# Gate and up projection of an encoder layer: 2x2 blocks with seven block products in place of eight

## The reference

```
h = modulate(rms_norm(x, g_pre_ffn), sh2, sc2)
f = (jax.nn.silu(h @ w_gate) * (h @ w_up)) @ w_down
x = x + gt2[:, None] * rms_norm(f, g_post_ffn)
```

## Time and profile before

| | |
|---|---|
| median of 3 runs | 1005.39 us (1005.0 to 1005.47) |
| profiled execution, first to last instruction (span) | 1003.3 us |
| its own time | not listed; the median lies 2.1 us above its span |
| gate and up, 40 chunks | 592.71 to 848.06 us of the span |
| busy: PE, DVE, ACT, POOL | 95%, 44%, 41%, 36% of the span |

### The profile page before, as it was taken

The page is one execution under the profiler, slowest core; times in us unless marked ns, Lnnn a source line. Parts: engine busy times, 40 slices in busy tenths (PEclk is TensorE's granted clock), DMA queues, the critical chain, the costliest instruction groups (busy, mean ns, idle before and its releaser), DMA issues. The chain is left out here.

```text
span 1003.3 us, 17736 instructions
## 1 busy us (share of the span) xinstructions
PE 954.9 (95%) x7104; PEld 908.1 (91%) x7104; DVE 436.6 (44%) x871; ACT 412.6 (41%) x771; POOL 365.1 (36%) x174
## 2 busy tenths in 40 slices
PE   3899999999999999999999899999999999999995
PEld 1698898999998999988888799999999999999995
DVE  5767559988884323432102743333333332000005
ACT  4755335465556555543333932222222223222221
POOL 2031016456453231244443044444444442434440
PEclk9999999999999999999999999999999999999998
DMA  9821031232131114357865032222222212222202
GB/s 363 319 99 48 8 107 71 102 105 92 67 120 53 36 43 151 146 204 277 286 209 163 1 105 85 84 84 84 82 84 71 79 61 86 87 88 87 81 36 95
DMA packets 35600, 111.61 MB, mean 111 GB/s; under 512 B 4240, under 2 KB 9360, under 8 KB 35280
## 3 DMA queue, kind: packets, MB, share of 16 engines
q1 hardware_dynamic: 31152, 102.48, 29.4%
q10 hardware_dynamic: 4112, 6.93, 1.8%
q0 software_dynamic: 272, 1.31, 0.3%
HBM read 100.38 MB, written 10.32 MB: 110 GB/s over the span
## 5 line engine op out<-in xcount | busy, mean ns | idle before, releaser
L1108 POOL TENSOR_TENSOR wlo<-raw,whi 128x1024 fp32r<-128x1024 f32 x52 | 128.6, 2473 | 233.3 <-ACT whi L744 223.9
L1163 POOL TENSOR_TENSOR wlo<-raw,whi 128x1024 fp32r<-128x1024 f32 x41 | 104.7, 2555 | 151.2 <-ACT whi L1071 151.2
L1875 PE MATMUL pj<-hh,wlo 128*128 128x288 f32 (+1 forms) x640 | 137.3, 296 | 0.0
L1875 PE MATMUL pj<-hh,whi 128*128 128x288 f32 (+1 forms) x640 | 137.0, 295 | 0.0
L1875 PE MATMUL pj<-hl,whi 128*128 128x288 f32 (+1 forms) x640 | 136.8, 295 | 0.0
L1631 PE MATMUL pj<-hh,whi 128*128 128x288 f32 x544 | 124.4, 310 | 5.4 <-ACT zs L825 2.4
L1631 PE MATMUL pj<-hh,wlo 128*128 128x288 f32 x544 | 117.7, 298 | 0.0
L1631 PE MATMUL pj<-hl,whi 128*128 128x288 f32 x544 | 117.1, 297 | 0.0
L1875 PEld LDWEIGHTS pj<-hh,wlo 128*128 128x128 f32 x640 | 103.4, 189 | 0.0
L1875 PEld LDWEIGHTS pj<-hh,whi 128*128 128x128 f32 x640 | 102.9, 188 | 0.0
L1875 PEld LDWEIGHTS pj<-hl,whi 128*128 128x128 f32 x640 | 102.8, 188 | 0.0
(11 more groups left out here) (226 smaller groups left out, 1992.0 us busy)
## 6 DMA issues: line engine op xcount, KB each, us to landing
raw<-in_w_s SPq DMA_DIRECT2D x94, 512.0 KB, 3.5
rawa<-in_w_ada SPq DMA_DIRECT2D x32, 512.0 KB, 6.2
rawd<-in_w_d SPq DMA_DIRECT2D x16, 704.0 KB, 4.0
raw<-in_w_ada SPq DMA_DIRECT2D x16, 512.0 KB, 10.2
g_raw<-gz ACTq DMA_DIRECT2D x16, 288.0 KB, 2.1
gate<-g_raw SPq DMA_DIRECT2D x8, 576.0 KB, 3.8
rawv<-in_w_v SPq DMA_DIRECT2D x8, 324.0 KB, 5.1
xt<-in_xT SPq DMA_DIRECT2D x2, 1152.0 KB, 6.8
```

What stands on the lines that cost most here:

```text
L1108: pool.tensor_tensor(rest, raw_of(c), whole.bitcast(F32), ALU.subtract).then_inc(w_lo, 1)
L1163: pool.tensor_tensor(wlo[:, slot(c), :], raw[:, raw_slot(c), :], whi[:, slot(c), :].bitcast(F32), ALU.subtract).then_inc(w_lo, 1)
L1875: ins = mm(pj[tile % 2][:, h, 0:HALF + 2 * h], w[:, slot(C_GU + q), b:b + P], x[h][:, kc, :], start=(kc == 0 and w is whi and x is hh2), s ...
```

## The change

The chunk pair of a tile is taken as 2x2 blocks: rows gate and up, columns the two halves of the contraction (A11, A12 of gate, A21, A22 of up, each 128 x 512 numbers); `h` as 2x2 blocks: rows the halves of the contraction, columns the two token halves (B11 to B22). The four blocks of the result (gate and up for each token half) come from seven block products of sums of blocks, each 4 blocks x 3 matmuls of 290 columns, in place of eight. Tiles 0 and 1 (four chunks, `N_STD`) stay as they were; the other 20 (`N_PAIR`) go the new way.

- DVE makes four sums of weight blocks a tile (`weight_sum`, 128 x 512), and once four sums of token blocks (`t_make`) and their low parts (`t_rest`); ACT makes the high parts of those (`t_split`).
- ACT and POOL split the seven weight operands of a tile, 128 x 512 each (`operand_hi`, and the loop on POOL), into a pair of slots of their own for each product (`op_hi[k]`, `op_lo[k]`).
- Each product has a bank of its own. ACT copies the first one out; DVE adds the others up (`gate_up`), multiplies by `rstd2` after that, and makes f with three multiply-adds.
- f of tiles 2 to 21 is kept whole (`fx`). Its high and low parts are made at the end of the stretch (`f_whole` on ACT, `rest_of_f` on DVE), in places that become free there.
- The loops of the stretch are written out; SP loads two chunks a tile into two pairs of raw slots; w_down has slots of its own, loaded when the last low part of the weights is made. The squares of the last norm go through three slots.

```diff
+PRODUCTS = (("A11", "B11"), ("S2", "T2"), ("A12", "B21"), ("S1", "T1"), ("S3", "T3"), ("A22", "T4"), ("S4", "B22"))
...
+        def operand_free(eng, i, k):
+
+            if i:
+                eng.wait_ge(st_full, made(i - 1, k))
...
+            for i in range(N_PAIR):
+                for m in range(2):
+                    if i < 2:
+                        sp.wait_ge(pj_full, full(T_OUT + KC - 1))
+                    else:
+                        sp.wait_ge(st_lo, made(i - 2, N_PROD - 1))
+                    sp.dma_start(sraw[:, 2 * (i % 2) + m, :], a["w_s"][S_OUT + KC + N_STD + 2 * i + m])\
+                      .then_inc(sraw_in[2 * (i % 2) + m], 16)
...
+            def operand_hi(i, k):
+
+                src = operand(act, i, k)
+                operand_free(act, i, k)
+                act.activation(op_hi[k][:, :], src, ACT.Copy).then_inc(st_hi, 1)
...
+            def copy_p1(i):
+
+                act.wait_ge(st_full, made(i, 0))
+                if i:
+                    act.wait_ge(c21_c22, i)
+                act.activation(vbuf[:, 1, :], tb[:, 0:HX], ACT.Copy).then_inc(p1_out, 1)
...
+            for i in range(N_PAIR):
+                if i:
+                    silu(i - 1)
+                copy_p1(i)
+                if i + 1 < N_PAIR:
+                    for k in range(N_PROD):
+                        operand_hi(i + 1, k)
+            hi_down(0, 0)
+            f_whole(0, 4)
             hi_down(0, 1)
+            f_whole(4, 12)
+            silu(N_PAIR - 1)
+            f_whole(12, FC)
...
+            for i in range(N_PAIR):
+                for k in range(N_PROD):
+                    src = operand(pool, i, k)
+                    pool.wait_ge(st_hi, made(i, k))
+                    operand_free(pool, i, k)
+                    pool.tensor_tensor(op_lo[k][:, :], src, op_hi[k][:, :].bitcast(F32), ALU.subtract).then_inc(st_lo, 1)
...
+            def weight_sum(i, j):
+
+                a11, a12, a21, a22 = (sraw_of(i, m, k) for m in range(2) for k in range(2))
+                x, y, op = ((a21, a22, ALU.add), (ssum[:, 0, :], a11, ALU.subtract), (a11, a21, ALU.subtract),
+                            (a12, ssum[:, 1, :], ALU.subtract))[j]
...
+            def f_made(t, gate_, up_):
+
+                v.wait_ge(sg_ready, t + 1)
...
+                    parts = [(fx[t][:, 0:NS], up_[:, 0, 0:NS], gate_[:, 0:NS], up_[:, 1, HALF + 1:HX]),
+                             (fx[t][:, NS:HALF], up_[:, 0, NS:HALF], gate_[:, NS:HALF], up_[:, 1, HALF:HALF + 1]),
+                             (fx[t][:, HALF:T], up_[:, 1, 0:HALF], gate_[:, HALF:T], up_[:, 1, HALF:HALF + 1])]
+                for to, x, y, shift in parts:
+                    ins = v.scalar_tensor_tensor(out=to, in0=x, scalar=shift, in1=y, op0=ALU.add, op1=ALU.mult)
...
+            def gate_up(i):
+
+                u2 = gbuf[:, 0, :].unsqueeze(1).to_broadcast([P, 2, HX])
+                v.wait_ge(p1_out, i + 1)
+                v.wait_ge(st_full, made(i, 2))
+                v.wait_ge(sg_ready, i + 2)
+                v.tensor_tensor(gbuf[:, 0:2, :], vbuf[:, 1, :].unsqueeze(1).to_broadcast([P, 2, HX]), lg[:, :, 0:HX],
+                                ALU.add).then_inc(u2_c11, 1)
+                if i:
+                    f_made(i + 1, gt, up)
+                if i < N_PAIR - 1:
+                    weight_sum(i + 1, 2)
+                    weight_sum(i + 1, 3)
+                else:
+                    rest_of_f(0, 6)
+                v.wait_ge(st_full, made(i, 4))
+                v.wait_ge(u2_c11, i + 1)
+                v.tensor_tensor(vbuf[:, :, :], u2, pj4[:, 1:3, 0:HX], ALU.add).then_inc(u4_u3, 1)
+                v.wait_ge(st_full, made(i, 5))
+                v.wait_ge(u4_u3, i + 1)
+                if i:
+                    v.wait_ge(f_ready, i + 2)
+                v.tensor_tensor(up[:, :, :], vbuf[:, 1, :].unsqueeze(1).to_broadcast([P, 2, HX]), pj4[:, 0:2, 0:HX],
+                                ALU.add).then_inc(c21_c22, 1)
+                v.wait_ge(c21_c22, i + 1)
+                v.tensor_tensor(up[:, :, 0:HALF], up[:, :, 0:HALF], two(rstd2[:, :]), ALU.mult).then_inc(up_ready, 1)
+                v.wait_ge(st_full, made(i, 6))
+                v.tensor_tensor(gbuf[:, 2, :], vbuf[:, 0, :], pvb[:, 0:HX], ALU.add).then_inc(c12_out, 1)
+                v.wait_ge(c12_out, i + 1)
+                v.tensor_tensor(two(gt[:, :]), gbuf[:, 1:3, 0:HALF], two(rstd2[:, :]), ALU.mult).then_inc(gt_ready, 1)
+                v.wait_ge(up_ready, i + 1)
+                if i + 2 < N_PAIR:
+                    weight_sum(i + 2, 0)
+                    weight_sum(i + 2, 1)
...
+            def product(i, k):
+
+                pe.wait_ge(st_lo, made(i, k))
+                bank = (tb, lg[:, 0, :], lg[:, 1, :], pj4[:, 1, :], pj4[:, 2, :], pj4[:, 0, :], pvb)[k]
+                if i:
+                    pe.wait_ge((p1_out, u2_c11, u2_c11, c21_c22, u4_u3, c21_c22, c12_out)[k], i)
...
+                for b in range(KH):
+                    for j, (w, x) in enumerate(((op_hi, 0), (op_hi, 1), (op_lo, 0))):
+                        ins = mm(bank[:, 0:HX], w[k][:, b * P:(b + 1) * P], moving[name][x][:, b, :],
+                                 start=(b == 0 and j == 0), stop=(b == KH - 1 and j == 2))
+                ins.then_inc(st_full, 1)
+
+            for i in range(N_PAIR):
+                for k in range(N_PROD):
+                    product(i, k)
+            pe.wait_ge(c21_c22, N_PAIR)
```

More of the change, by code:

```diff
@@ L53 @@
 BLK_DOWN = FC // 2
+KH = KC // 2
+N_STD = 4
+N_PAIR = FC - N_STD // 2
+HX = HALF + 2
 QCOL = [0] + [NS + P * i for i in range(4)]
@@ L283, in build @@
         wlo, _ = sb("wlo", [P, RING, 1024], F32R)
[L285 to L288, removed]
         h_off = at["x"]
@@ L291, in build @@
         hl, _ = sb("hl", [P, KC, T], F32R)
[L292 to L295, removed]
+        at["x"] += 4 * KC * 2 * 4
+        off_l2 = h_off + 2 * KC * HX * 4
+        xres = [sb(f"xres{h}", [P, KC, HALF], where=off_l2 + h * KC * HX * 4)[0] for h in range(2)]
         A0 = at["x"]
@@ L549, in wait_used @@
                 tile = tile_of[c]
-            eng.wait_ge(pj_full, full(tile) if turns is None else turns * chunks + full(tile))
+            eng.wait_ge(pj_full, full(tile))
         def slot_free(eng, c):
@@ L1052, in hi_down @@
             def hi_down(d, k):
                 act.wait_ge(down_in[k], 16 * (d + 1))
[L1054 to L1079, removed]
+                if d:
+                    wait_down(act, d - 1, k)
+                else:
+                    act.wait_ge(st_lo, made(N_PAIR - 1, N_PROD - 1))
+                    act.wait_ge(st_full, made(N_PAIR - 1, k))
+                act.activation(dhi[k][:, :], rawd[:, k, :], ACT.Copy).then_inc(d_hi, 1)
+            def f_whole(t0, t1):
+                for t in range(t0, t1):
+                    act.wait_ge(f_ready, t + 1)
+                    act.wait_ge(st_full, made(N_PAIR - 1, FH_AFTER[t]))
+                    act.activation(fh[t][:, :], fx[t][:, :], ACT.Copy).then_inc(f_hi, 1)
@@ L1517, in _ @@
                     inverse(rstd1, 0, 1)
-                half_lo(h, 5, 6, 7)
+                    half_lo(h, 5, 6, 7)
+                else:
+                    for j in range(3):
+                        half_lo(h, 5 + j)
+                        weight_sum(0, j)
             def first_half(h):
@@ new lines, in _ @@
+            inverse(rstd2, 1, 0)
+            first_half(0)
+            t_make(0)
+            t_make(1)
+            inverse(rstd2, 1, 1)
+            first_half(1)
+            t_make(2)
+            weight_sum(0, 3)
+            v.wait_ge(pj_dve, taken(T_GU + 1, "D"))
+            f_made(0, sg, ft)
+            t_make(3)
+            t_rest(0)
+            n = T_GU + 2
+            v.wait_ge(pj_full, full(n))
+            v.wait_ge(f_ready, 1)
+            v.tensor_tensor(two(sg[:, :]), pj_view(n), two(rstd2[:, :]), ALU.mult)
```

380 lines of the change are left out of this document (254 added, 126 removed).

## The result

The changed kernel takes 1032.72 us (median of 4 runs, 1031.35 to 1033.42), the kernel before 1005.21 beside it (1005.0 to 1005.47): a ratio of 1.0272, 95% interval 1.0257 to 1.0286. The forecast was 1036.0. The profiled execution has a span of 1030.6 us against 1003.3, so 27.3 us have to be found.

The account below looks back on a forecast made before the run. VectorE, taking turns with GpSimd's low parts, was to set the tiles' pace instead of TensorE. Span 1003.3 + 16.2 (tiles) + 13.5 (seam) + 1.7 (clock) = 1034.7, plus 2.1 around it, 1036.8; forecast 1036 us, range 1004 to 1050.

Parts of the forecast that it names:

- The matmuls: In the 20 tiles: seven products for eight, 84 matmuls of 133.0 ns, 1.60 us less a tile, 31.9 us over all.
- The turn: VectorE's round per tile: 5.95 us of waits behind low parts plus 7.7 of own work, 13.7 us; given 70%.
- The stretch: The 20 gate and up tiles: 13.8 + 11.2 + 18 x 13.7 = 271.6 us against 255.35, +16.2 us.
- The seam: Ahead of the down projection: TensorE stands 13.7 us, with splits of f queued before two PSUM sums on VectorE; +13.5 us.
- The clock: Behind the wait ahead of the down projection: half of 3.4 us at half clock, +1.7 us; inside tiles hidden by waits.
- least port time: Per tile, GpSimd low parts (8.05 us) and VectorE operations with two SBUF inputs (4.1) taking turns without gaps: 12.15 us.
- the locked order of three engines: In the tiles: silu waits for VectorE, high parts queue behind silu, so low parts start with the multiply-adds; 13.7 us, not 12.15.
- TensorE keeping the pace: Rival in the tiles: low parts and two-input operations hardly meet, 11.2 us a tile, 977 us in all; 8%.
- The packed port: Rival in the tiles: the three multiply-adds go through together, VectorE's round about 12.4 us, 1013 us in all; 16%.
- Everything colliding: Rival in the tiles: all seven low parts stand in VectorE's way, 16.7 us a tile, 1100 us in all; 6%.

Follow-up runs that it names:

- e1_no_low: Changed kernel with GpSimd writing zeros in place of the weights' low parts from the second of the 20 tiles on: 984.8 us, ratio 0.9802.
- e2_seam: Changed kernel with the first six splits of f behind the last two PSUM sums in VectorE's queue: 1029.18 us, ratio 1.0239.
- e4: Changed kernel with the seven low parts of a tile made by VectorE instead of GpSimd from the second tile on: 1003.11 us, ratio 0.9976.
- v6: Changed kernel with prompt silu, up sum and C12 in PSUM, half the gate scaling reading PSUM, early splits of f behind the last tile's work: 983.87 us.
- e3: Changed kernel with ScalarE writing silu of the prompt tokens to PSUM, where two multiply-adds read it: 1004.3 us, ratio 0.9993.
- e5_order: Changed kernel with ScalarE's silu of a tile behind the first two high parts of the next: 1042.68 us, ratio 1.0369.

## Why the prediction was right, step by step

**The matmuls.** 1680 came, at 133.9 ns (11.25 us a tile in e1_no_low) where 133.0 was taken. Right within 0.1 us a tile, and off the path, as the forecast had it.

**The turn.** Forecast 13.7 us, measured 13.56 to 13.62 from the third turn on. Its inside fits as well: the waits over the price alone are 1.03 + 1.04 + 1.03 us for the multiply-adds (1541, 1486, 1309 less 512, 446, 280), 2 x (1250 - 685) = 1.13 for S3, 1.02 for the scaling of up and 0.60 for that of gate: 5.85 us where 5.95 stood in the sum. What is left, 7.74, is the own work taken as 7.7; the 0.2 us for marks in it, for which the forecast had no row, compare with 0.25 us a turn in which VectorE is not busy at all. Low parts and two-input operations at their full durations, 9.0 and 5.4 us, would add up to 14.4 us a turn, which did not come: the small overlaps seen in the earlier trace rows counted. That TensorE waits for the last PSUM sum ahead of the fourth product was right too; in tiles that ran at full clock the trace lists 1.76 us of idle time there (about 0.55 in those that had half clock before it). Start to start a tile is 13.59 - 11.25 = 2.34 us longer than its matmuls, and 2.5 was forecast. In many tiles some 0.26 us of that stands ahead of the first product, where the weight load does wait for GpSimd's low part (eight times from 640 to 810 us, 2.4 us in all); it costs nothing, as the fourth product has to wait anyway.

**The stretch: right mechanism, too long.** Forecast +16.2 us, measured +12.0. Of the 4.2 us: the first product began at 590.76, 1.95 us ahead of the 592.71 from which I counted. That is no gain of the change but chance: in the seven other versions, with the same work ahead, it began anywhere from 590.8 to 593.4. Up to the fourth product it took 6.36 us for the 4.8 of three products, as the second one waited 1.26 us for its block sum, which the sum did not have (+1.6). The first turn took 12.93 for 13.8 (-0.9): the sixth product waited 1.44 us where the term said 2.6, so the start waited 2.7 us in two places where the term had 2.6 in one. The second turn took 12.29 for 13.7 (-1.4): the lag had not built up yet. Seventeen turns at 13.59 for 13.7 are -1.8, the last four products +0.3.

**The seam.** Forecast 13.7 us of standing, measured 13.54. Its parts came as listed: first low part 861.98 to 865.15, first split behind it to 865.76, second low part to 868.78 with a split behind it, the others to 872.07, the two sums to 873.59. e2_seam shows what the order is worth: not all 13.5, but 7.8 at the first wait and 3.5 in the end.

**The clock.** +1.7 was forecast behind the seam, half of the 3.4 us at a granted clock of 0.50 in the earlier trace rows; that it would last as long behind the seam no row showed. The down projection took 2.1 longer. The term was too small, as the half clock lasted 5.7 us there (0.51 from 873.64 to 879.40). Inside the tiles the forecast let the clock fall into time that is waited anyway. That held: in five tiles it was at half for 3.4 us (0.50 from 637.0 to 640.4), and the turn stayed at 13.6.

**A reason that stays open.** The forecast laid the gap between the least port time (12.15) and the turn (13.7) on the locked order of three engines, low parts let go just when the multiply-adds start. GpSimd does wait for high parts, 49.4 of 170 us. The runs don't part order from load. e1, e4 and v6 shorten the turn by taking readers off the port. In e3 the port time falls too, but most of the gain is a smaller gap above it, and GpSimd waits for 12.0 of 170 us: that speaks for the order. e5_order, the one run that changes the order alone, moved the standing time to VectorE and lost 0.55 us a tile. Whether a better order exists was not tried.

**The rivals.** TensorE keeping the pace (11.2 us a tile) is what e1 and v6 reach by removing or thinning out the meeting, not what the change does. The packed port (12.4) would have needed the multiply-adds to go through together; the timeline has a low part's wait at each of the three. Everything colliding (16.7) would have had seven waits; there are six, the last a partial one.

## What to carry to other kernels

Before work is moved to an idle GpSimd, look whether its instructions read SBUF beside operations of VectorE with both inputs in SBUF: here such operations stood 5.85 us of a 13.6 us turn behind low parts (a multiply-add of 64 elements took 1309 ns for 280), and the busy shares of the old profile, 36% and 44%, said nothing about it. The remedies, by what they gave here: put one operand in PSUM (1032.7 to 1004.3 us with silu alone; to 983.9 with two more places and the later splits), or give the work to the engine that is waited for anyway, if its price there is below the waits it causes (4.2 us of work for 5.9 of waits: 1003.1). When waits are moved by an order, look at the next operation in line before counting them as won.

## What was not expected of the hardware

After 13.5 us without matmuls the half clock lasted 5.7 us into the down projection, where one 2.70 us stretch before had 3.4 us in all. The windows of the changed kernel around the seam's end:

```profile
873.64:879.40 5.76, 5.76 (x24) 5.76 (x25) 5.73 (x9) 3.83 (x8) 0.00 (x0) 0.51 0.00 0
879.40:890.00 10.60, 10.60 (x82) 10.60 (x82) 7.82 (x14) 5.75 (x9) 3.14 (x1) 1.00 0.00 0
```

24 matmuls in 5.76 us are 240 ns each, against 133 at full clock. In the stretch the clock fell in five of the twenty tiles of this execution (at 637, 664, 692, 719 and 746 us) and in none of e2_seam (granted clock 1.00 from 592.70 to 861.50), whose turns are as long; why is open. ScalarE's silu of 512 elements was no dearer into PSUM than into SBUF: 673 ns in e3_silu_psum against 708 in the changed kernel (640 to 810 us).
